# A hybrid decoder's state-space step rewritten: double-buffered scan rows, scans two quarters apart, weight remainders in halves

## The chip, the cores and the metric

The kernel runs on one core of a Trainium2 chip. The metric is device time in microseconds (us) of one execution, the median of a few runs. The engines are TensorE (PE in the profile, its weight loads PEld), VectorE (DVE), ScalarE (ACT), GpSimd (POOL) and SyncE (SP); each runs its own instructions in order and waits on counting semaphores.

## The reference, cut to what matters

One inference step of a hybrid decoder with 2 layers, model width 1024, over 512 prompt tokens and 8 x 4 sample tokens (544 columns in all), in float32. Each layer projects x, mixes a state-space branch with an attention branch, and adds an MLP. The change concerns the state-space branch (32 heads of 64, 8 groups, state 128, chunks of 128 tokens):

```python
xbc, conv_new = causal_depthwise_conv(xbc, conv_buf, conv_w, conv_b)   # width 4, then SiLU
dt = softplus(dt_raw + dt_bias); a = -exp(a_log)
acum = cumsum(dtc * a)                      # within a chunk
decay = exp(where(causal, acum_i - acum_j, -inf))
y_diag = einsum(cb * decay, x * dt)         # cb = C B^T in the chunk
states = einsum(B, x * dt * exp(acum_end - acum))
h <- h * exp(acum_end) + states             # chunk after chunk
y_off = einsum(C, h_prev) * exp(acum)
y = (y_diag + y_off + d_skip * x) * silu(z)
out = y * rsqrt(mean(y * y over a group) + eps) * norm_g
```

The sample tokens do the same from stored states (8 sequences, one chunk of 32 columns), which are updated and written out.

## The kernel before

Activations lie transposed, features on partitions and the 544 tokens on columns. A weight tile of 1024 x 128 is a **unit** (170 a layer), loaded by SyncE into a ring of four slots. For near-float32 products from fast passes ScalarE rounds it (`high`, L887, into `whi`), GpSimd takes the remainder (`low`, L1661, into `wlo`), and TensorE makes three products for each of eight slices and two column halves: high x high, high x low, low x high (L413, L414, L416). A unit is thus 48 matmuls of 272 columns, and each needs `low` of its unit (`w_split`) and, at the end, an eviction by ScalarE (`evac`, L894) that frees its accumulator.

Stages of a layer: the q, k, v projections, attention, **the state-space groups**, the merge of the branches with gates, the output projection, the MLP. In the groups' stage a step handles two groups at once: six units of group g are projected (B, C, two tiles of x, two of z) while the scan of group g - 1 runs in between. Step 0 has only the projection (the attention's sample tokens run in between), steps 1 to 7 have both, the last step has only the scan, with two units of the gates. `all_groups` calls `group(...)` once a step on every engine; steps 2 to 7 stand in a hardware loop of three rounds with two steps each.

TensorE's order is fixed: after every second slice of a unit (a **quarter**, 12 matmuls, 24 quarters a step) `between()` may insert a piece of the scan. `turn(c)` transposes chunk c's x and B into PSUM bank X[0] and makes C B^T there; `scan(c)` multiplies it out (L736, L739) and adds the chunk's state product (L748). Then come `turn_y`, `new_states` (L764), `rms` (L773) and `spread` (L780) at the quarters in the constants below.

VectorE's `chunk(k)` in order: C times decay (`cea`, L1434); from X[0] the rows x*dt (`xdt`, L1444), x*dt*decay (`xde`, L1445), B (`btok`, L1447) and the masked C B^T (`cbm`, L1451), which frees X[0]; the mask times the decays (`mdec`, L1455), which releases `scan(k)`; after that scan the state `hst` (L1465, four instructions). `conv(q)` is three taps (L1413) for each of four tiles, `silu(q)` L1420 and L1425; then `y_prompt` (L1477), `gate_z` (L1483), `y_sample`, `y_carried` (L1500), `gated_y` (L1505), `decay_states` (L1510) and `add_states` (L1516) for the samples, `norm_inverse` (L1520), `norm_scale` (L1525). ScalarE starts the convs (L1012), makes their tanh (L1018), the decays (`decay`, L1025 and L1029; `ea`, L1058), the squares (L1046) and the root (L1050). GpSimd, besides the remainders, pads each conv tile with its stored columns (`pad_of`, L1741 to L1744) and issues the loads and stores of states and tables.

The three orders that matter, as they stand:

```python
SCAN_AT = (3, 5, 8, 10, 12); Y_TURN_AT = 14; NEW_AT = 16; RMS_AT = 19; SPREAD_AT = 22
# TensorE: turn(0) of the next group waits for rs_ready, rms waits for sq_ready and ns_add
# VectorE: chunk(0) chunk(1) conv(0) chunk(2) chunk(3) y_prompt chunk(4) gate_z conv(1) silu(0)
#   y_sample y_carried gated_y silu(1) decay_states conv(2) add_states silu(2)
#   norm_inverse conv(3) silu(3) norm_scale
```

Of the kernel before, what the change touches and what calls it, by code (L numbers as in the profile page):

```python
# [30 lines left out]
P = 128  # L31
DEPTH, D = 2, 1024
SEQ, NB, NS = 512, 8, 4
TS = NB * NS
# [8 lines left out]
REG = 23840  # L43
# [33 lines left out]
SCAN_AT = (3, 5, 8, 10, 12)  # L77
Y_TURN_AT = 14
NEW_AT = 16
RMS_AT = 19  # L80
SPREAD_AT = 22
# [21 lines left out]
def build(nc, A):  # L103

    with ExitStack() as ctx:
# [55 lines left out]
        gconv = sb("gconv", [P, 20])  # L161
        gt = sb("gt", [P, NC + 1, 3, HG])
# [61 lines left out]
        xdt = reg.take(256)  # L224
# [5 lines left out]
        xde = reg.take(256)  # L230
        btok = reg.take(P)
# [15 lines left out]
        gates = reg.take(2, T)  # L247
        reg.restart(after_stores)
# [26 lines left out]
        def bc(ap, n):  # L275
# [30 lines left out]
        gp_ready, post_init, conv_done, th_ready, post_ready, spad_ready, thz_ready, zs_done = (  # L306
            sem(n) for n in ("gp_ready", "post_init", "conv_done", "th_ready", "post_ready", "spad_ready",
                             "thz_ready", "zs_done"))
        ea_ready, gt_ready, e_ready, t_done, x0_free, m_ready, y_done, h_ready = (
            sem(n) for n in ("ea_ready", "gt_ready", "e_ready", "t_done", "x0_free", "m_ready", "y_done", "h_ready"))  # L310
# [3 lines left out]
        ns_done, ns_add = (sem(n) for n in ("ns_done", "ns_add"))  # L314
# [68 lines left out]
        def _(pe):  # L383
# [138 lines left out]
            with pe.Fori(0, DEPTH) as L:  # L522
# [235 lines left out]
                def new_states(s):  # L758

                    pe.wait_ge(y_evac, 2 * s + 2)  # L760
                    for e in range(2):
                        for q in range(4):
                            rows = slice(32 * q, 32 * q + 32)
                            mm = nc.tensor.matmul(X[q][:, e * 256:(e + 1) * 256], bm[rows, e, :], xde[rows, :],  # L764
# [111 lines left out]
        def _(act):  # L876
# [67 lines left out]
            with act.Fori(0, DEPTH) as L:  # L944
# [59 lines left out]
                def group(g, s, unit0, rounds, late):  # L1004

                    c = None if g is None else L * GROUPS + g

# [960 lines left out]
```

## Time and profile before

| what | value |
|---|---|
| median of 3 runs | 3051.59 us (3051.0 to 3053.08) |
| the profiled execution | 3047.54 us |
| its span, first to last instruction | 3045.8 us |
| TensorE matmuls, weight loads busy | 2710.5, 2545.6 us (89%, 84%) |
| VectorE, ScalarE, GpSimd busy | 1296.3, 1087.7, 1052.0 us (43%, 36%, 35%) |
| mean granted TensorE clock | 0.944 |
| seven steps with scan and projection, a layer | 439.0 us |

The profiled execution is one run under the hardware profiler; the 1.7 us beside its span lie around the instructions. Busy shares are means over stages that differ. The granted clock is the share of full speed that the chip gave TensorE.

### The profile page before, as it was taken

The numbers are of one execution on the slowest core, as the hardware profiler recorded it, in microseconds if no ns is written. First come the engines' busy times: TensorE is split into PE (matmuls) and PEld (weight loads), VectorE is DVE, ScalarE is ACT, GpSimd is POOL, SyncE is SP. The second block draws the span as 40 slices with busy tenths as digits, with TensorE's granted clock in tenths as the row PEclk, the third lists the DMA queues.
The fourth block names the chain that finished last, engine by engine and source line by source line (L and its number), as shares of the span: only waits on it lengthen the run. The fifth ranks groups of instructions, "written<-read, shape, count | busy, mean of one in ns | idle before, by whom it ended". The sixth has DMA issues, their size and how long they took to land.

```text
span 3045.8 us, 53838 instructions
## 1 busy us (share of the span) xinstructions
PE 2710.5 (89%) x21264; PEld 2545.6 (84%) x21264; DVE 1296.3 (43%) x2064; ACT 1087.7 (36%) x1557; POOL 1052.0 (35%) x749
## 2 busy tenths in 40 slices
PE   5978888888889999999879798888887999999996
PEld 5966678788779989999879667778786999899996
DVE  4253367666641262011252524776676313520213
ACT  2232344455332243132232413445544322431323
POOL 3311233343233343434343012333332433433433
PEclk9989999999989999999989899999998999999998
DMA  3222322243222223222222232333333222223222
GB/s 118 83 101 95 108 94 96 94 137 107 89 72 83 88 70 90 84 89 90 70 74 81 86 118 92 97 101 123 108 96 102 74 88 81 75 84 90 86 88 78
DMA packets 66770, 280.47 MB, mean 92 GB/s; under 512 B 8384, under 2 KB 8832, under 8 KB 60064
## 3 DMA queue, kind: packets, MB, share of 16 engines
q1 hardware_dynamic: 51312, 184.51, 19.8%
q0 software_dynamic: 15280, 93.40, 8.5%
q8 instruction: 134, 2.20, 0.3%
q14 instruction: 44, 0.36, 0.0%
HBM read 248.81 MB, written 29.07 MB: 91 GB/s over the span
## 4 chain that ended last, share of the span: by engine, by line
PE 74%; DVE 15%; issue 3%; DVEq 3%; ACT 2%; ACTq 1%; DMA 1%; POOL 1%; POOLq 0%; SPq 0%
PE acc L413 19%; PE acc L414 19%; PE acc L416 19%; DVE region L1413 5%; PE px L736 1%; PE px L748 1%; PE acc L642 1%; PE px L677 1%; DVE region L1516 1%; PE px L597 1%; DVEq L1453 1%; PE acc L573 1%; DMA wring<-in_wst 1%; DVE region L1510 1%; PE acc L837 1%
## 5 line engine op out<-in xcount | busy, mean ns | idle before, releaser
L1661 POOL TENSOR_TENSOR wring_parts<-wring,whi 128x1024 fp32r<-128x1024 f32 x343 | 835.4, 2437 | 1063.3 <-ACT whi L887 1042.2
L413 PE MATMUL acc<-xhi,whi 128*128 128x272 f32 x3552 | 1008.6, 301 | 3.8 <-ACT big L948 2.7
L414 PE MATMUL acc<-xlo,whi 128*128 128x272 f32 x3552 | 974.9, 293 | 0.0
L416 PE MATMUL acc<-xhi,wring_parts 128*128 128x272 f32 x3552 | 746.6, 292 | 0.0
L413 PEld LDWEIGHTS acc<-xhi,whi 128*128 128x128 f32 x3552 | 686.3, 193 | 26.5 <-issue 19.6
L414 PEld LDWEIGHTS acc<-xlo,whi 128*128 128x128 f32 x3552 | 685.1, 193 | 3.5
L887 ACT ACTIVATE whi<-wring 128x1024 fp32r<-128x1024 f32 x343 | 362.0, 1056 | 888.1 <-DMA wring<-in_wst 797.3
L416 PEld LDWEIGHTS acc<-xhi,wring_parts 128*128 128x128 f32 x3552 | 566.9, 192 | 0.0
L413 PE MATMUL acc<-region_parts,whi 128*128 128x272 f32 x1792 | 487.3, 291 | 14.5 <-DVE big_parts L1585 14.5
L414 PE MATMUL acc<-big_parts,whi 128*128 128x272 f32 x1536 | 416.1, 289 | 0.0
L416 PE MATMUL acc<-region_parts,wring_parts 128*128 128x272 f32 x1792 | 372.2, 289 | 0.0
L413 PEld LDWEIGHTS acc<-region_parts,whi 128*128 128x128 f32 x1792 | 340.2, 190 | 16.0 <-issue 16.0
L414 PEld LDWEIGHTS acc<-big_parts,whi 128*128 128x128 f32 x1536 | 292.0, 190 | 0.0
L416 PEld LDWEIGHTS acc<-region_parts,wring_parts 128*128 128x128 f32 x1792 | 283.0, 190 | 0.0
L894 ACT ACTIVATE region<-acc 128x544 f32<-128x544 f32 x172 | 106.3, 618 | 395.4 <-PE acc L416 393.1
L1413 DVE SCALAR_TENSOR_TENSOR region<-region,gconv 128x600 f32<-128x600 f32 x192 | 205.3, 1069 | 19.7 <-ACT region L1012 6.2
L1625 DVE TENSOR_TENSOR region<-region 128x544 f32<-128x544 f32 x64 | 48.6, 760 | 269.9 <-ACT region_parts L1133 269.9
L1741 POOL COPY region<-region 128x32 f32<-128x32 f32 x64 | 29.2, 457 | 351.5 <-ACT region L894 347.4
L1018 ACT ACTIVATE region<-region 128x600 f32<-128x600 f32 x64 | 44.9, 702 | 183.1 <-DVEq L1415 183.1
L1025 ACT ACTIVATE region<-region,gt 128x128 f32<-128x128 f32 (+1 forms) x320 | 96.4, 373 | 15.2 <-DVE region L1455 11.0
L736 PE MATMUL px<-region 128*64 128x128 f32 (+1 forms) x640 | 63.2, 288 | 41.6 <-DVE region L1455 40.7
L1465 DVE SCALAR_TENSOR_TENSOR region<-region,px 128x64 f32<-128x64 f32 x192 | 41.1, 276 | 117.3 <-PE px L748 117.3
(233 smaller groups left out, 3104.5 us busy)
## 6 DMA issues: line engine op xcount, KB each, us to landing
wring<-in_wst SPq DMA_DIRECT2D x343, 512.0 KB, 3.6
region<-scratch_ac POOLq DMA_DIRECT2D x16, 1088.0 KB, 7.1
region<-in_st POOLq DMA_DIRECT2D x16, 1024.0 KB, 5.0
out_stout<-region POOLq DMA_DIRECT2D x16, 1024.0 KB, 9.0
big<-in_kc POOLq DMA_DIRECT2D x16, 768.0 KB, 5.6
big<-in_vc POOLq DMA_DIRECT2D x16, 768.0 KB, 5.7
out_kv<-region POOLq DMA_DIRECT2D x2, 3264.0 KB, 10.4
region<-in_x SPq DMA_DIRECT2D x1, 2176.0 KB, 8.4
```

The source lines that it names most:

```text
L413: nc.tensor.matmul(o, w_hi_, hi, start=first, stop=False)
L414: nc.tensor.matmul(o, w_hi_, lo, start=False, stop=False)
L416: mm = nc.tensor.matmul(out[:, 512 * h:512 * h + HT], w_lo_, parts(h)[0], start=False, stop=last)
L736: mm = nc.tensor.matmul(out, xdt[0:n, hcols], mdec[0:n, hh, 0:n], start=True, stop=c in (0, NC))
L887: nc.scalar.activation(whi[:, slot, :], whole[:, slot, :], ACT.Copy).then_inc(w_hi[slot], 1)
L894: nc.scalar.activation(halves(out), two(acc[b]), func, **kw).then_inc(acc_free[b], 1)
L1018: nc.scalar.activation(th[:, q % 2, 0:CONVW], pre[:, q % 2, 0:CONVW], ACT.Tanh).then_inc(th_ready, 1)
L1025: nc.scalar.activation(seg[0:n, k % 2, hh, 0:n], acb[0:n, hh, k * CHUNK:k * CHUNK + n], ACT.Relu, bias=gt[0:n, k, 1, hh:hh + 1], scale=-1.0)
L1413: nc.vector.scalar_tensor_tensor(v, raw[:, q, tap:tap + CONVW], gconv[:, 4 * q + tap:4 * q + tap + 1], v, ALU.mult, ALU.add)
L1465: ins = nc.vector.scalar_tensor_tensor(hst[:, hcols], hst[:, hcols], ea[:, hh, last:last + 1], X[3][:, hcols], ALU.mult, ALU.add)
L1625: nc.vector.tensor_tensor(v, v, v, ALU.mult)
L1661: pool.tensor_tensor(wlo[:, slot, :], whole[:, slot, :], whi[:, slot, :].bitcast(F32), ALU.subtract)\
```

## The change

Five things are done together. (1) The scan pieces stand at other quarters, `rms` and `spread` now ahead of `new_states`, and other waits go with them: `rms` no longer waits for `ns_add`, `turn(0)` of the next group does, `new_states` waits for `yssm_ready`. (2) `xdt`, `xde` and `btok` have two buffers each; a chunk is split into `rows_of` (what leaves X[0], and the decayed state `hdec`), `carry_state` of the chunk before, and `factors_of`. VectorE's and ScalarE's orders are rewritten; ScalarE makes the first two decays of the next scan at the end of a step. (3) The per-group copies `gt` and `gconv` are gone: the engines read `tokm` and `par` in place, `par` being halved once a layer. (4) The loop over steps is written out, so that slices are constants. (5) On GpSimd the remainders are made in halves of 512 columns (`low_half`), each behind a hold on an event of the scan, in a new order.

The constants and the loop over steps:

```diff
-SCAN_AT = (3, 5, 8, 10, 12)
-Y_TURN_AT = 14
-NEW_AT = 16
-RMS_AT = 19
-SPREAD_AT = 22
+SCAN_AT = (2, 4, 6, 8, 11)
+Y_TURN_AT = 13
+RMS_AT = 15
+SPREAD_AT = 18
+NEW_AT = 20
...
-            with eng.Fori(0, GROUPS // 2 - 1) as i:
-                group(2 * i + 2, first + 2 * i + 1, U_GRP + 12, 3 * i, True)
-                group(2 * i + 3, first + 2 * i + 2, U_GRP + 18, 3 * i, True)
+            for g in range(2, GROUPS):
+                group(g, first + g - 1, U_GRP + 6 * g, 0, True)
```

TensorE, in `turn`, `scan`, `new_states` and `rms`:

```diff
                         if late:
-                            pe.wait_ge(rs_ready, s)
+                            pe.wait_ge(ns_add, s)
...
+                    xdt, xde, btok = xdt2[c % 2], xde2[c % 2], btok2[c % 2]
                     pe.wait_ge(m_ready, 5 * s + c + 1)
-                    if c == 0 and late:
-                        pe.wait_ge(yssm_ready, 2 * s)
...
-                    pe.wait_ge(y_evac, 2 * s + 2)
+                    pe.wait_ge(yssm_ready, 2 * s + 2)
...
                     pe.wait_ge(sq_ready, s + 1)
-                    pe.wait_ge(ns_add, s + 1)
```

ScalarE; before, `decay(0)`, `ea` and `decay(1)` stood at a step's head. A step with scan and projection now runs: `zs`, decay(2), tile(0), decay(3), conv_init(0), decay(4), tile(1), conv_init(1), conv_act(0), copy_y, tile(2), conv_act(1), conv_init(2), square, root, tile(3), conv_act(2), conv_init(3), first_decay, conv_act(3), tile(4), rest_of_decay, tile(5).

```diff
+                    def first_decay():
+                        act.wait_ge(acb_ld, 16 * c + 16)
+                        if s is not None:
+                            act.wait_ge(m_ready, 5 * c)
+                        decay(0, g)
+
+                    def rest_of_decay():
+                        if s is not None:
+                            act.wait_ge(st_decayed, c)
+                        nc.scalar.activation(ea, acb, ACT.Exp).then_inc(ea_ready, 1)
+                        decay(1, g)
...
                 act.wait_ge(yssm_ready, 16 * L + 16)
+                act.wait_ge(ns_add, 8 * L + 8)
```

VectorE. A step now runs: chunks 0 to 3, conv(0), chunk(4), y_prompt, gate_z, conv(1), silu(0), y_sample, y_carried, gated_y, silu(1), conv(2), norm_inverse, silu(2), norm_scale, decay_states, conv(3), silu(3), add_states. `factors_of` holds what is left of the old chunk: `cea`, then `mdec`.

```diff
+                    def rows_of(k):
...
+                        dve.wait_ge(t_done, 5 * s + k + 1)
+                        xt = X[0][:, 0:256].rearrange("p (h d) -> p h d", h=HG)
+                        for out, j in ((xdt, 0), (xde, 2)):
+                            nc.vector.tensor_tensor(out.rearrange("p (h d) -> p h d", h=HG), xt,
+                                                    bc(tokm[:, k, j, gs * HG:(gs + 1) * HG], HD), ALU.mult)
...
+                        dve.drain().then_inc(x0_free, 1)
+                        if k > 1:
+                            last = k * CHUNK - 1
+                            nc.vector.tensor_tensor(hdec.rearrange("p (h d) -> p h d", h=HG),
+                                                    hst.rearrange("p (h d) -> p h d", h=HG),
+                                                    ea[:, :, last:last + 1].to_broadcast([P, HG, HD]), ALU.mult)
+                            dve.drain()
+
+                    def carry_state(k):
+
+                        dve.wait_ge(y_done, 5 * s + k + 1)
+                        if k > 0:
+                            nc.vector.tensor_tensor(hst, hdec, X[3][:, 0:256], ALU.add).then_inc(h_ready, 1)
+                        else:
+                            dve.wait_ge(h_free, s + 1)
+                            nc.vector.tensor_copy(hst, X[3][:, 0:256]).then_inc(h_ready, 1)
...
+                    def chunk(k):
+
+                        rows_of(k)
                         if k > 0:
+                            carry_state(k - 1)
+                        factors_of(k)
```

GpSimd. `last` is the unit that the third projection of the step uses; the units u to u + 4 plus AHEAD (3) are those after it. Behind the lines shown, the remainder of u + 1 + AHEAD waits for `m_ready` of chunk 4, the store of `hst` for `h_ready`, `load_decay` for `e_ready` (then pad 2, u + 2 + AHEAD, pad 3), u + 3 + AHEAD for `rs_spread`, u + 4 + AHEAD for the last `post_ready`, and the store of the sample states for `ns_add`.

```diff
+            def low_half(L, u, h):
+
+                slot, use = unit(L, u)
+                if h == 0:
+                    pool.wait_ge(w_hi[slot], use + 1)
+                cols = slice(h * KT * P // 2, (h + 1) * KT * P // 2)
+                ins = pool.tensor_tensor(wlo[:, slot, cols], whole[:, slot, cols], whi[:, slot, cols].bitcast(F32),
+                                         ALU.subtract)
+                if h == 1:
+                    ins.then_inc(w_split[slot], 1)
...
+                    if late:
+                        hold(pool, st_st, 16 * s)
+                        load_state(gs, s)
...
+                    last = U_GRP + 6 * gs + 5 + AHEAD
+                    for h in range(2):
+                        hold(pool, t_done, 5 * s + h + 1)
+                        low_half(L, last, h)
                     if projects:
                         pad_of(g, 0)
+                        for h in range(2):
+                            hold(pool, t_done, 5 * s + h + 3)
+                            low_half(L, u + AHEAD, h)
                         pad_of(g, 1)
...
```

## Rows read from the trace of the kernel before

**Rows 1.** The page: busy time; a group (busy, mean ns); a DMA issue.
```profile
PE 2710.5 (89%) x21264; PEld 2545.6 (84%) x21264; DVE 1296.3 (43%) x2064; ACT 1087.7 (36%) x1557; POOL 1052.0 (35%) x749
...
L1413 DVE SCALAR_TENSOR_TENSOR region<-region,gconv 128x600 f32<-128x600 f32 x192 | 205.3, 1069 | 19.7 <-ACT region L1012 6.2
...
out_stout<-region POOLq DMA_DIRECT2D x16, 1024.0 KB, 9.0
```

**Rows 2.** Windows: length, each engine's busy us (instructions), clock, DMA share, GB/s.
```profile
365.40:804.40 439.00, 378.82 (x3263) 352.40 (x3264) 302.64 (x553) 219.81 (x367) 158.25 (x161) 0.94 0.30 101
1873.70:2312.70 439.00, 379.77 (x3263) 353.62 (x3264) 303.37 (x553) 219.55 (x366) 157.91 (x161) 0.94 0.31 101
...
1123.00:1461.00 338.00, 337.46 (x2685) 337.20 (x2684) 61.82 (x81) 105.00 (x127) 139.36 (x61) 1.00 0.29 87
...
558.50:562.00 3.50, 3.50 (x17) 3.50 (x18) 1.84 (x5) 3.43 (x6) 0.56 (x1) 0.53 0.59 195
```

**Rows 3.** Waits of TensorE, 365.4 to 804.4: total us, times, longest.
```profile
PE px L773 <- DVE region L1516: 24.9, 7, 3.6
PE px L736 <- DVE region L1455: 17.1, 11, 2.3
...
PE px L711 <- DVEq L1453: 9.7, 7, 2.5
PE px L711 <- issue: 8.0, 2, 4.1
```

**Rows 4.** Timeline of VectorE, 505 to 575: start, us, instruction, [idle before].
```profile
509.04 2.85 DVE L1455 TENSOR_TENSOR region<-region 128x512 f32<-128x512 f32 x1
515.23 0.86 DVE L1465 SCALAR_TENSOR_TENSOR region<-region,px 128x64 f32<-128x64 f32 x4 [3.35 <-PE px L748]
...
517.87 0.69 DVE L1455 TENSOR_TENSOR region<-region 128x512 f32<-128x512 f32 x1
...
524.41 0.42 DVE L1444 TENSOR_TENSOR region<-px,gt 128x256 f32<-128x256 f32 x1
...
527.11 4.65 DVE L1413 SCALAR_TENSOR_TENSOR region<-region,gconv 128x600 f32<-128x600 f32 x3
...
533.95 1.29 DVE L1505 TENSOR_TENSOR region<-region 128x1088 f32<-128x1088 f32 x1
...
538.31 2.69 DVE L1413 SCALAR_TENSOR_TENSOR region<-region,gconv 128x600 f32<-128x600 f32 x3 [0.16 <-issue]
...
572.32 0.86 DVE L1465 SCALAR_TENSOR_TENSOR region<-region,px 128x64 f32<-128x64 f32 x4 [2.21 <-PE px L748]
```

**Rows 5.** Timeline of GpSimd, same stretch.
```profile
508.33 0.20 POOL L1742 COPY region<-cst 128x24 f32 x1
...
508.99 2.35 POOL L1661 TENSOR_TENSOR wring_parts<-wring,whi 128x1024 fp32r<-128x1024 f32 x1 [0.30 <-issue]
...
570.98 2.38 POOL L1661 TENSOR_TENSOR wring_parts<-wring,whi 128x1024 fp32r<-128x1024 f32 x1 [0.65 <-issue]
```

**Rows 6.** The chain that ended last, 440 to 505: start, us, what.
```profile
500.59 0.33 PE px L711 x3
...
502.21 0.64 PE px L748 x2
```

**Rows 7.** Timeline of ScalarE, 505 to 575.
```profile
535.27 1.11 ACT L1046 ACTIVATE region<-region 128x1088 f32<-128x1088 f32 x1 [1.61 <-DVE region L1505]
...
541.67 1.04 ACT L887 ACTIVATE whi<-wring 128x1024 fp32r<-128x1024 f32 x1
...
545.36 1.28 ACT L1050 ACT_TABLE_LOAD   x1
546.66 0.37 ACT L1050 ACTIVATE region<-px,eps 128x136 f32<-128x136 f32 x1
```

**Rows 8.** Timeline of ScalarE and GpSimd, 804 to 872.
```profile
850.61 8.86 ACT L1112 ACTIVATE region_parts<-big 128x544 fp32r<-128x544 f32 x16 [4.82 <-DVE big L1525]
...
849.65 0.54 POOL L1673 DMA_DIRECT2D wdt<-in_wdt  x1 [4.38 <-DMA out_stout<-region]
```

More of the change, by code:

```diff
@@ L42 @@
 CW = 4
-REG = 23840
+REG = 23880
 D_IN = HEADS * HD
@@ L223, in build @@
         cea = cea_flat.rearrange("p (h n) -> p h n", h=HG)
-        xdt = reg.take(256)
+        xdt2 = [reg.take(256) for _ in range(2)]
+        btok2 = [reg.take(P)]
         assert reg.at <= after_masks
@@ L247, in build @@
         gates = reg.take(2, T)
+        xde2.append(reg.take(256))
+        hdec = reg.take(256)
         reg.restart(after_stores)
@@ L1413, in conv @@
                             nc.vector.scalar_tensor_tensor(v, raw[:, q, tap:tap + CONVW],
-                                                           gconv[:, 4 * q + tap:4 * q + tap + 1], v, ALU.mult, ALU.add)
+                                                           par[:, g, 4 * q + tap:4 * q + tap + 1], v, ALU.mult, ALU.add)
                             dve.drain()
@@ L1543, in group @@
                     elif g is None:
-                        for k in range(NC):
+                        for k in range(NC + 1):
                             chunk(k)
                         y_prompt()
-                        chunk(NC)
                         gate_z()
@@ L1570, in group @@
                         silu(1)
+                        conv(2)
+                        norm_inverse()
+                        silu(2)
+                        norm_scale()
                         decay_states()
-                        conv(2)
-                        add_states()
-                        silu(2)
-                        norm_inverse()
                         conv(3)
                         silu(3)
-                        norm_scale()
+                        add_states()
                 all_groups(dve, L, group)
@@ L1750, in group @@
                     projects, scans = g is not None, s is not None
-                    if scans:
-                        if late:
-                            hold(pool, st_st, 16 * s)
-                            load_state(GROUPS - 1 if g is None else g - 1, s)
-                        if projects:
-                            hold(pool, cout_st, 16 * (L * GROUPS + g))
-                    if projects and not scans:
-                        pool.memset(raw[:, :, 0:PAD], 0.0)
+                    if not scans:
+                        pool.memset(raw[:, :, 0:PAD], 0.0)
+                        for q in range(4):
+                            pad_of(g, q)
+                        load_decay(g, L * GROUPS + g)
+                        load_state(g, L * GROUPS + g)
+                        low(L, u + 3 + AHEAD)
+                        low(L, u + 4 + AHEAD)
+                        return
@@ L1769, in group @@
+                        for h in range(2):
+                            low_half(L, u + 1 + AHEAD, h)
+                    hold(pool, h_ready, 4 * s + 4)
+                    pool.dma_start(row(A["hout"], s, "o p n -> (o p) n"), hst).then_inc(h_st, 16)
                     if projects:
+                        hold(pool, e_ready, 5 * s + 5)
+                        load_decay(g, L * GROUPS + g)
                         pad_of(g, 2)
-                        if scans:
-                            low(L, u + 2 + AHEAD, rounds)
+                        for h in range(2):
+                            low_half(L, u + 2 + AHEAD, h)
@@ L1789, in group @@
+                    hold(pool, ns_add, s + 1)
+                    pool.dma_start(row(A["stout"], s, "o p b n -> (o p) b n"), st).then_inc(st_st, 16)
+                    if not projects:
                         hold(pool, st_st, 16 * s + 16)
```

154 lines of the change are left out of this document (60 added, 94 removed).

## The prediction

> **What bounds the kernel now.** I read the page first: TensorE is busy 89% of the span [rows 1], so only stretches in which it is not can give time. The windows show which [rows 2]. In the feed-forward stretch it works without a gap at the full granted clock, 2685 matmuls in 338.0 us, 0.126 us each. The seven steps of the group loop that carry both a scan and a projection (groups 1 to 7, twice, once a layer) take 439.0 us a layer, 62.7 us each, at a mean granted clock of 0.94.
>
> How short could such a step be? It has 288 projection matmuls: 288 x 0.126 = 36.3 us. Between them stand the scan's own pieces. A step of turn and scan at full clock goes from 500.59 to 502.85, 2.26 us [rows 6]; there are three like it, and I put the other seven pieces, which carry fewer or shorter matmuls, at 1 us each (estimate from the same rows). Together 36.3 + 6.8 + 7.0 = 50.1 us. So 12.6 us per step are lost. The waits of TensorE say where [rows 3]: over seven steps 24.9 us at L773 (the squares' sum, which waits for the state update L1516), 17.1 at L736 and 9.7 at L711 (a scan and a turn, both for VectorE), 8.0 at the loop's back edge ("issue", 4.1 at the longest). That is 59.7 of the 88 us; the rest is the clock: after the wait at 558.5 the granted clock is 0.53, the lower of the two levels (1.2 and 2.4 GHz), for 3.5 us [rows 2].
>
> So TensorE waits for VectorE, although VectorE is busy only 302.64 / 439 = 69%, 43.2 us a step [rows 2]. Two things make it late. One is the order. The other is GpSimd: the multiply L1455 takes 0.69 us at 517.87 but 2.85 us at 509.04, where the remainder L1661 ran on GpSimd from 508.99 for 2.35 us; a conv triple takes 2.69 us at 538.31 and 4.65 us at 527.11 [rows 4, 5]. L1465, which reads PSUM, takes 0.86 us at 515.23 and the same at 572.32, amid a remainder that began at 570.98.
>
> **The change, part by part.** I set up one step with t = 0 at its first turn. A quarter is 12 matmuls, 1.51 us.
>
> *Scans two quarters apart.* Turn 3 starts after six quarters, turn 0 (0.55), turn 1 with scan 0 (2.26 less 0.5 for the state's matmuls) and turn 2 with scan 1 (2.26): 9.06 + 4.6 = 13.7, done at 14.2. Scan c needs, after scan c-1, one state add (0.4, the size of L1444), the C product and the mask multiply (0.7 each, one shape), 1.8 us of VectorE [rows 4], since the turned rows are now made beforehand in buffers of their own; TensorE spends 3.0 us on two quarters meanwhile. So I expect the waits at L711 and L736 to go, and cost the double buffers at nothing; their cover is 1.2 us, and a remainder half (below) can eat it. The four L1465 (0.86) become one product hdec and one add, about 0.8 with its drain.
>
> *VectorE from there to the gate.* Chunk 3 takes as long as now, 3.3 us from 515.23 to the end of 517.87's multiply. Then conv 0 (2.8), then chunk 4 up to the gated y: now 524.41 to 535.24 is 10.8 us; I take off the 1.96 that GpSimd added to the 4.65 conv, and add hdec with the carry (0.8) and y_prompt (1.4, now ahead of it): 11.1 [rows 4]. With 0.3 a time for a few handovers G, the end of the gate, is 14.3 + 3.3 + 2.8 + 11.1 + 0.8 = 32.3. TensorE reaches the squares' sum (quarter 15) at 22.6 + 11.1 (the pieces before it, by the same rows) = 33.8, and needs G plus the square (1.1 and a handover): even.
>
> *After the gate.* The new order releases the sum without the state update, so the wait at L773, 3.6 us a step, loses its reason. What is late next: silu 2 waits for its tanh, and ScalarE now has between them the square 1.1, a table load 1.28, the root 0.37, a weight copy 1.0, an eviction (0.6, put at that from its shape, half the square's), the load back 1.28 and the tanh (0.7, likewise): G + 6.4 with a handover [rows 7]. Then, by the rate of rows 4 (256 elements in 0.42, 1088 in 1.29: 0.15 us and 1.05 ns an element), silu 0.9, norm_scale 1.5, decay_states 2.3, conv 3 2.7, its tanh on ScalarE 0.8, silu 0.9, add_states 2.3: 11.4. I add 1.7 for a spread that comes late at the lower clock and a remainder half ahead of decay_states: 19.5. The next step's turn 0 waits for exactly that add (ns_add), and behind turn 0 stands the whole in-order projection. So a step is 32.3 + 19.5 = 51.8 us plus what GpSimd adds before G.
>
> The Trainium skill ("ScalarE: Activation LUTs", section "What ACT_TABLE_LOAD costs") puts a switch at 1283 ns of load and about 1380 ns of DRAIN. The trace agrees with the first figure alone: the load at 545.36 lasts 1.28 us and the root starts at 546.66. By the page's 2.66 us each step would be 2.8 us longer and the kernel 39 us; by the row it is not.
>
> *The remainders in halves.* The work is the same, 2.35 us a unit, and a second fixed cost: the smallest copies take 0.20 [rows 5], so a half is 1.2 to 1.3 us. Between t = 14 and G three units run, six halves, with two pads. Best case all fall on PSUM reads of VectorE: 0. Worst, each blocks a full 1.25: 7.5. Now the 12 conv taps of a step take 1.069 us on average [rows 1] against 0.90 (2.69 / 3), so GpSimd adds at least 2.0 a step. The holds on t_done do little for the first two units: GpSimd stands at the store of the sample states until it lands (9.0 us from issue [rows 1]), and by then those events are past. I take 2.7, near today's level. A step: 54.5 us.
>
> Against the change speaks that hdec reads two SBUF tiles where L1465 read PSUM: a new op that GpSimd can hold up, three times a step. The Trainium skill ("SBUF — State Buffer", section "SBUF: two separate sides") states it as a rule: the shared port pair goes to one of the two for the whole instruction when the VectorE op has two SBUF inputs. By it 3 x 1.25 = 3.8 us a step at worst, which is the third rival's price.
>
> *Queued behind the new waits.* On GpSimd, pad 0 and the remainders wait behind the stores' holds: unit 2's remainder is due at t = 21.5 and comes at about 13.5 (the store, the next load's issue, two halves), 8 us of cover. On ScalarE tile 4's eviction now stands behind conv 3's tanh, at t = 49, and is due at the next step's first projection, 2 us later; a longer VectorE chain moves both. In group 0, tile 4 waits for the first decay (five activations, the size of the root's 0.37 and one larger: 2 us [rows 7]), which delays the first projection of group 1: I take +2 us a layer.
>
> *Tables in place, loops written out.* gt and gconv, two VectorE ops of 60 and 20 columns, go; they lay in front of chunk 0, where TensorE did not wait for them. Two back edges a layer go, already counted in the 62.7. Halving par once costs one small VectorE op beside ScalarE's staging; without that cover 0.5 us.
>
> *Last step (no projection).* VectorE has no convs and the scans come sooner; adding the same lengths, ScalarE may start on the gated output about 39 us after the first turn, against 46.2 now (850.61 - 804.4) [rows 8]. GpSimd's next remainders still wait for the store of the states (landed at 849.65 now), so I take 6 of the 7: -12 us for both layers.
>
> **Sum.** 14 steps x (62.7 - 54.5) = 115; + 12 - 4 = 123 us. The profiled execution took 3047.5 us: 2924.5. The median of the runs is 4 us above it: **2928 us**.
>
> **Rivals.** (1) TensorE bound: GpSimd falls into PSUM reads and waits, c near 0, a step of 51: 14 x 11.7 + 8 = 172, 2880 us. For it: VectorE's 43 us fit; against: no slack is left anywhere. (2) Contention as priced by the worst half of the range, or hdec held up each time: a step of 58, 14 x 4.7 + 8 = 74, 2978 us. For it: the 2.85 and 4.65 us rows. (3) The waits only move, from L773 to the same sum waiting for the gate and to turn 0: a step of 60, 46 us, 3006 us. (4) Slower: turn 0 on ns_add closes a ring through VectorE's whole work; if the 22.6 us of GpSimd (158.25 / 7) nearly all stand in its way, 43.2 + 20 = 63 to 64 us a step, 3062 us; it decides from 11 us of contention a step, four times what I take.
>
> **Numbers.** Chances: my forecast 0.45, (1) 0.22, (2) 0.20, (3) 0.07, (4) 0.06. The range takes in the steps from 50 to 59 us, all but (3) and (4): 2866 to 2990. 0.2%, 6 us, is about what a measurement can tell from no change. Faster 0.94, same 0.01, slower 0.05.
>
> **What would show it.** Right: no wait at the back edges; no or short waits at scans and turns 1 to 4; the sum's wait under 3.5 us and released by ScalarE's square; turn 0 of each step released by the state add; a mean granted clock above 0.94 in the steps; steps of 53 to 56 us. Wrong: turn 0 waiting for nothing (then rival 1); conv taps above 1.07 us on average (rival 2); a projection waiting for its remainder or for an eviction, which would break the cover I gave to GpSimd's and ScalarE's queues.

## The result, and the profile after

The changed kernel took 2938.44 us (median of 4 runs, 2934.34 to 2943.11); the kernel before took 3051.3 us beside it (4 runs, 3037.03 to 3053.08). The ratio is 0.964, with a 95% interval of 0.9608 to 0.9673: faster, and 10 us above the 2928 that was forecast, inside the range. The profiled execution took 2938.64 us, with a span of 2937.1.

The windows of the seven steps of each layer, to be held against the first two of [rows 2]:

```profile
364.20:753.90 389.70, 365.38 (x3263) 340.95 (x3264) 297.45 (x497) 222.27 (x369) 172.47 (x202) 0.97 0.32 113
1818.20:2207.70 389.50, 365.21 (x3263) 340.75 (x3263) 296.79 (x497) 222.30 (x370) 172.67 (x202) 0.97 0.32 113
```

The step went from 62.7 to 55.7 us (779.2 / 14), at a mean granted clock of 0.97 in place of 0.94, with the same 3263 matmuls. The two stretches give 98.8 us. The waits of TensorE over the whole execution show what is left (columns as in [rows 3]; over the whole execution of before, L773 had 57.7 us in 16 waits, L736 40.7 in 23, the two waits at L711 20.2 and 16.2):

```profile
PE px L771 <- ACT region L1046: 36.9, 16, 3.5
...
PE px L711 <- DVE region L1544: 13.7, 14, 1.0
...
PE acc L413 <- POOL wring_parts L1678: 6.7, 2, 3.4
...
PE px L735 <- DVE region L1490: 4.6, 5, 1.1
PE acc L413 <- ACT region L892: 3.6, 4, 1.2
```

The wait for the state update at the squares' sum has gone; the sum (now L771) waits for ScalarE's square L1046 instead, up to 3.5 us. Scans (now L735) wait 4.6 us in all. The back edges are no longer in the list. Each step's turn 0 (L711) waits for the state add L1544, 0.97 us as a rule. The page's lines for VectorE's conv, GpSimd's halves and ScalarE's conv_init:

```profile
L1687 POOL TENSOR_TENSOR wring_parts<-wring,whi 128x512 fp32r<-128x512 f32 x172 | 272.8, 1603 | 217.0 <-issue 74.4
...
L1426 DVE SCALAR_TENSOR_TENSOR region<-region,par 128x600 f32<-128x600 f32 x192 | 206.6, 1076 | 36.8 <-ACT region L1011 23.2
...
L1011 ACT ACTIVATE region<-region,par 128x600 f32<-128x600 f32 x64 | 56.5, 882 | 88.4 <-POOLq L1773 88.4
```

The conv taps are as slow as before (1076 ns against 1069 in [rows 1]): there, contention with GpSimd has not gone down. And a line that was not foreseen: L1011 waits 88.4 us for L1773, the drain behind GpSimd's pad copies. The chain that ended last shows what that does. One step's second half (start, us, what):

```profile
729.04 3.75 POOLq L1773
...
732.82 0.89 ACT region L1011
733.70 1.01 ACT region L1046
...
734.76 0.96 PE px L771 x16
...
736.24 0.23 PE acc L414
...
741.66 0.94 PE px L778 x8
...
744.10 2.20 DVE region L1538
...
746.49 1.59 DVE region L1426
...
748.16 0.84 DVE region L1426
...
749.99 0.71 ACT region L1017
...
750.73 0.69 DVE region L1433
...
751.52 2.21 DVE region L1544
...
753.87 0.30 PE px L711
```

Read it from the top. GpSimd's queue is at the drain for 3.75 us; then ScalarE can do conv_init, and only behind it, in order, the square; then the sum. The matmuls after the sum, behind TensorE's wait, take 0.23 us each until 738.65, where the full granted clock has 0.126 [rows 2]. The windows before and after that moment have the granted clock (third figure from the end): 0.53, the lower level, and 1.00:

```profile
735.70:738.60 2.90, 2.90 (x15) 2.90 (x14) 2.71 (x3) 1.62 (x3) 0.26 (x1) 0.53 0.00 0
738.70:741.60 2.90, 2.90 (x25) 2.90 (x24) 0.24 (x1) 2.87 (x4) 1.08 (x4) 1.00 0.57 178
```

So the spread at L778 is late twice over: by the sum's delay, and by the matmuls at the lower clock. From there it is VectorE's series to the state add and turn 0, as forecast, with conv taps of 1.59 among those of 0.84.

Why is the drain so long? GpSimd and ScalarE in the step from 644.09 to 698.57:

```profile
668.55 3.59 POOL L1687 TENSOR_TENSOR wring_parts<-wring,whi 128x512 fp32r<-128x512 f32 x2 [2.80 <-DVE region L1490]
...
672.64 0.54 POOL L1758 DMA_DIRECT2D region<-scratch_ac  x1
...
675.59 0.21 POOL L1772 COPY region<-region 128x35 f32<-128x35 f32 x1
679.11 3.05 POOL L1687 TENSOR_TENSOR wring_parts<-wring,whi 128x512 fp32r<-128x512 f32 x2 [3.31 <-issue]
```
```profile
679.01 0.89 ACT L1011 ACTIVATE region<-region,par 128x600 f32<-128x600 f32 x1 [3.57 <-POOLq L1773]
679.81 1.09 ACT L1046 ACTIVATE region<-region 128x1088 f32<-128x1088 f32 x1
680.92 1.28 ACT L1050 ACT_TABLE_LOAD   x1
682.21 0.37 ACT L1050 ACTIVATE region<-px,eps 128x136 f32<-128x136 f32 x1
```

The pad's last copy ends at 675.80, yet ScalarE is released at 679.01. What stands ahead in GpSimd's queue is the load of the decay table, issued at 672.64. The view of that one load (L1758, 672 to 674) has its landing:

```profile
DMA to landing us min/median/max: 6.2/6.2/6.2
```

That is at 678.85, and the drain ends at 678.98. It is so in every step. The traces of the changed kernel, of its second run and of e2 to e10 have 213 pads at whose last copy a load issued by GpSimd was still under way: each drain ended 0.13 to 0.21 us after that load had landed, and the landings came from 5.0 to 8.3 us after the issue. So the drain goes by the landing, not by a time of its own. The load in its turn stands behind a pair of halves that took 3.59 us.

The last step of a layer, where ScalarE starts on the gated output (before: 46.2 us after the first turn, [rows 8]):

```profile
793.94 8.88 ACT L1123 ACTIVATE region_parts<-big 128x544 fp32r<-128x544 f32 x16 [4.69 <-DVE region L1544]
```

That is 40.1 us after its first turn at 753.87, 6.2 us sooner than before (6.17 from unrounded times), twice. With the 98.8 from the steps that makes 111.1; the profiled executions differ by 3047.5 - 2938.64 = 108.9, so some 2.2 us were lost elsewhere: from that start to the next layer's first turn 0, and to the end, the changed kernel is 1.2 and 2.4 us longer, and ahead of the first turn 0 it is 1.2 us shorter. The wait for a remainder in the list above (L413 for L1678, 3.4 us a layer, in the merge) is new, but no loss: with the 8.0 us for VectorE there it makes 14.7, and before TensorE waited 14.5 there for VectorE alone.

### The profile page after: what moved, and what is told of

The parts are those of the page before. It is cut to its first block, busy times and chain, and to the rows that moved or that the text cites. A ratio compares the mean times of both kernels' runs of the same rounds, so it can differ in the third digit from the quotient of the medians.

```text
span 2937.1 us, 53722 instructions
## 1 busy us (share of the span) xinstructions
PE 2681.7 (91%) x21264; PEld 2521.7 (86%) x21264; DVE 1275.6 (43%) x1938; ACT 1070.1 (36%) x1545; POOL 1080.1 (37%) x835
## 4 chain that ended last, share of the span: by engine, by line
PE 77%; DVE 11%; ACT 3%; issue 2%; POOLq 2%; POOL 1%; ACTq 1%; DMA 1%; DVEq 1%; SPq 0%
PE acc L413 20%; PE acc L414 20%; PE acc L416 19%; DVE region L1426 2%; POOLq L1773 2%; PE px L677 1%; PE acc L642 1%; PE px L735 1%; PE px L747 1%; DVE region L1544 1%; PE px L597 1%; PE acc L573 1%; DVE region L1538 1%; PE acc L458 1%; PE acc L835 1%
## 5 line engine op out<-in xcount | busy, mean ns | idle before, releaser
L413 PE MATMUL acc<-xhi,whi 128*128 128x272 f32 x3552 | 999.6, 299 | 6.9 <-ACT region L892 3.6
L1678 POOL TENSOR_TENSOR wring_parts<-wring,whi 128x1024 fp32r<-128x1024 f32 x257 | 625.2, 2435 | 978.2 <-ACT whi L885 973.3
L413 PEld LDWEIGHTS acc<-xhi,whi 128*128 128x128 f32 x3552 | 677.6, 191 | 29.7 <-issue 22.5
L413 PE MATMUL acc<-region_parts,whi 128*128 128x272 f32 x1792 | 488.7, 291 | 14.8 <-DVE big_parts L1602 8.0
L413 PEld LDWEIGHTS acc<-region_parts,whi 128*128 128x128 f32 x1792 | 341.2, 190 | 17.5 <-issue 10.3
L1687 POOL TENSOR_TENSOR wring_parts<-wring,whi 128x512 fp32r<-128x512 f32 x172 | 272.8, 1603 | 217.0 <-issue 74.4
L1426 DVE SCALAR_TENSOR_TENSOR region<-region,par 128x600 f32<-128x600 f32 x192 | 206.6, 1076 | 36.8 <-ACT region L1011 23.2
L1025 ACT ACTIVATE region<-region,tokm 128x128 f32<-128x128 f32 (+1 forms) x320 | 96.2, 372 | 19.6 <-DVE region L1490 19.6
L1448 DVE TENSOR_TENSOR region<-px,tokm 128x256 f32<-128x256 f32 x160 | 60.6, 420 | 98.3 <-PE px L717 94.5
L1011 ACT ACTIVATE region<-region,par 128x600 f32<-128x600 f32 x64 | 56.5, 882 | 88.4 <-POOLq L1773 88.4
L1651 DVE SCALAR_TENSOR_TENSOR region<-region,acc 128x544 f32 x16 | 11.5, 721 | 175.8 <-PE acc L416 175.8
```

Source lines behind the costliest of these rows:

```text
L413: nc.tensor.matmul(o, w_hi_, hi, start=first, stop=False)
L1011: nc.scalar.activation(pre[:, q % 2, 0:CONVW], raw[:, q, PAD:RAWW], ACT.Identity, bias=par[:, g, 16 + q:17 + q], scale=par[:, g, 4 * q + 3 ...
L1025: nc.scalar.activation(seg[0:n, k % 2, hh, 0:n], acb[0:n, hh, k * CHUNK:k * CHUNK + n], ACT.Relu, bias=tokm[0:n, k, 1, head:head + 1], sca ...
L1426: nc.vector.scalar_tensor_tensor(v, raw[:, q, tap:tap + CONVW], par[:, g, 4 * q + tap:4 * q + tap + 1], v, ALU.mult, ALU.add)
L1448: nc.vector.tensor_tensor(out.rearrange("p (h d) -> p h d", h=HG), xt, bc(tokm[:, k, j, gs * HG:(gs + 1) * HG], HD), ALU.mult)
L1678: pool.tensor_tensor(wlo[:, slot, :], whole[:, slot, :], whi[:, slot, :].bitcast(F32), ALU.subtract)\
```

## The experiments

All times are ratios to the kernel before, run on the same chip. "Step" is the mean over the 14 steps that scan and project. Kernels e2 to e10 are edits of the changed kernel, e1 of the kernel before.

**The loop alone (e1).** Before, with the groups' loop written out:

```diff
-            with eng.Fori(0, GROUPS // 2 - 1) as i:
-                group(2 * i + 2, first + 2 * i + 1, U_GRP + 12, 3 * i, True)
-                group(2 * i + 3, first + 2 * i + 2, U_GRP + 18, 3 * i, True)
+            for g in range(2, GROUPS):
+                group(g, first + g - 1, U_GRP + 6 * g, 0, True)
```

> The kernel before with one part of the change alone: the loop over steps 2 to 7 written out. My theory: the four back edges (two a layer) cost 4.1 us of idle TensorE each and some 1.7 us more at the lower clock after it, so this alone is 23 us faster than before, ratio 0.992, with no wait on 'issue' left at L711. Rival: written-out code has to be fetched just the same, the wait turns up elsewhere: ratio 1.000.

Measured: 0.9925 (0.9901 to 0.9949). No back edge is left among the waits, and the sum's wait is what it was (57.8 us in 16). The loop is worth 0.75% by itself.

**Whole remainders (e2), halves without their holds (e3), no remainder at all (e4).** In e2 each pair of halves is one whole remainder; where each half had its own hold, it stands behind both. e3 keeps the halves and drops the five waits that release them. e4 fills the halves with zeros: TensorE's work stays, the group products lack this part, and GpSimd reads nothing.

```diff
 e2 (at four places so; at the first two the holds of both halves stay ahead of it)
-                        for h in range(2):
-                            low_half(L, u + 1 + AHEAD, h)
+                        low(L, u + 1 + AHEAD)
 e3
-                        hold(pool, t_done, 5 * s + h + 1)
-                            hold(pool, t_done, 5 * s + h + 3)
-                        hold(pool, m_ready, 5 * s + 5)
-                        hold(pool, rs_spread, s + 1)
-                        hold(pool, post_ready, 4 * (L * GROUPS + g) + 4)
 e4
-                    pool.wait_ge(w_hi[slot], use + 1)
+                    hold(pool, w_hi[slot], use + 1)
...
-                ins = pool.tensor_tensor(wlo[:, slot, cols], whole[:, slot, cols], whi[:, slot, cols].bitcast(F32),
-                                         ALU.subtract)
+                ins = pool.memset(wlo[:, slot, cols].bitcast(F32), 0.0)
```

> The changed kernel with whole remainders (1024 columns) at the same releases, halves undone. My theory: a remainder in VectorE's way now blocks up to 2.4 us where a half blocks 1.25, about 1 us more a step in the ring from turn 3 to the state add: 14 us slower than the changed kernel, ratio to before 0.969. Rival 1: the lock's total is the same, nothing changes: 0.964. Rival 2: the halves are what made the ring short, 4 us a step: 56 us slower, 0.982.

> The changed kernel with the halves not held back by scan events (the holds on t_done, m_ready, rs_spread and post_ready ahead of the remainders are gone). My theory: the t_done holds are past when GpSimd comes to them and the others move a half by little: within 10 us of the changed kernel, ratio to before 0.961 to 0.967. Rival: the holds keep GpSimd out of VectorE's two-input work; without them 3 us a step, 42 us slower, 0.978.

> The changed kernel with the halves of the remainder replaced by a fill with zeros, which reads no SBUF (the remainders of the weights used in the groups' stage are left out of the products). My theory: GpSimd costs the ring 2.7 us a step; with that gone the conv triples fall to 2.7 us each, a step to 52.5 to 53 us, the kernel by 38 to 45 us, ratio to before 0.950. Rival: the ring is set by ScalarE's chain and handovers, VectorE has the room to take GpSimd's blocks: 10 us at most, 0.961.

Measured: e2 0.9648 (0.9616 to 0.9681), e3 0.9619 (0.9588 to 0.9651), e4 0.9492 (0.9462 to 0.9523). Neither halving nor the releases gave anything beyond the uncertainty of the comparison; my 14 us for halving fell. e4 came out as expected, with a step of 52.2 (51.4 to 51.5 for most). What is left at turn 0 and at the sum is 0.2 us each time and 13.8 us in 16, half of that in the two last steps:

```profile
PE px L771 <- ACT region L1046: 13.8, 16, 3.4
...
PE px L711 <- DVE region L1544: 3.2, 14, 0.2
```

So the remainders cost 3.4 us a step. (A fill takes GpSimd 0.53 us and a half 1.29, medians, so e4 takes away GpSimd's time as well as the contention.) To see where, take mean ns of one instruction from VectorE's groups, for the operations that read SBUF alone (of `mdec` the four prompt chunks); the column before the last is their busy time beyond e4's, over the execution:

| kernel | conv L1426 | silu L1433 | hdec L1460 | cea L1481 | mdec L1490 | gate_z L1511 | gated L1533 | decay L1538 | beyond e4, us | step, us |
|---|---|---|---|---|---|---|---|---|---|---|
| e4 | 867 | 692 | 427 | 684 | 737 | 1285 | 1293 | 2285 | 0 | 52.2 |
| after | 1076 | 691 | 460 | 764 | 887 | 1285 | 1292 | 2284 | 55 | 55.7 |
| e2 | 880 | 861 | 755 | 716 | 943 | 2227 | 1292 | 3243 | 74 | 55.4 |
| e3 | 867 | 1447 | 654 | 1110 | 994 | 1284 | 1323 | 2285 | 96 | 54.7 |
| e6 | 995 | 690 | 510 | 709 | 841 | 1284 | 3440 | 2285 | 71 | 56.1 |
| e8 | 867 | 1356 | 663 | 1233 | 770 | 1285 | 3316 | 2284 | 115 | 58.5 |
| e9 | 871 | 692 | 466 | 684 | 737 | 1284 | 1296 | 2446 | 5 | 52.3 |

e3 has 41 us more contention than the changed kernel and is no slower. What an instruction is held up by counts only where the step has no slack. Ahead of the gate VectorE's wait for the turned y makes up for it: 0.37 us of that wait are left in the changed kernel, 1.4 in e4 (medians), and the gated y starts 32.1 us after turn 0 in both; in e3 part of the delay gets through, and it starts at 32.9. Between gate and state add nothing makes up for it.

**The quarters (e5).** The changed kernel with the old places of turns and scans:

```diff
-SCAN_AT = (2, 4, 6, 8, 11)
-Y_TURN_AT = 13
-RMS_AT = 15
-SPREAD_AT = 18
-NEW_AT = 20
+SCAN_AT = (3, 5, 8, 10, 12)
+Y_TURN_AT = 14
+RMS_AT = 16
+SPREAD_AT = 19
+NEW_AT = 21
```

> The changed kernel with the scan pieces back at the old distances (3, 5, 8, 10, 12; then 14, 16, 19, 21), all engines' orders as changed. My theory: VectorE's serial stretch starts at turn 3, which moves from quarter 6 to quarter 8, 3.0 us later, and the ring to the state add is full, so a step grows by 2 to 3 us: 28 to 42 us slower than the changed kernel, ratio to before 0.974 to 0.978. Rival: the order on VectorE is the whole gain, TensorE's quarters have room: 0.964.

Measured: 0.9845 (0.9811 to 0.988), a step of 59.6: right in sign, and about twice the size expected. The rows of turn 3 start 18.5 us after turn 0 instead of 14.4 (medians of L1448), and the step is 3.9 us longer, so all four microseconds arrive at the end. VectorE does not use the time: it waits for each turn, and the new waits are at the end of the ring:

```profile
PE px L771 <- ACT region L1046: 54.8, 16, 5.3
PE px L711 <- DVE region L1544: 34.8, 14, 2.5
```

**The load of the decay table behind pad 2 (e6), the state add ahead of silu 3 (e7).**

```diff
 e6
+                        pad_of(g, 2)
                         hold(pool, e_ready, 5 * s + 5)
                         load_decay(g, L * GROUPS + g)
-                        pad_of(g, 2)
 e7
                         conv(3)
+                        add_states()
                         silu(3)
-                        add_states()
```

> The changed kernel with one move on GpSimd: the load of the next decays is issued after pad 2 instead of ahead of it. In the changed kernel's trace the drain behind pad 2 takes 3 us longer than behind pad 1, with that load issued 2.4 us before it, and ScalarE's conv start 2 and then the square wait for it (the square starts at 679.8 where its input was there at 678.3). My theory: the drain waits for the load's descriptors; without it the square starts some 1.2 us earlier and a step is 0.9 to 1.2 us shorter: 13 to 17 us faster than the changed kernel, ratio to before 0.959. Rival: the drain is late because VectorE holds the port during conv 1; the move does nothing: 0.964.

> The changed kernel with VectorE's state add ahead of silu 3, so that it runs while ScalarE makes the tanh that silu 3 waits for (0.8 us). My theory: the ring from the gate to the next turn 0 is full (each turn 0 waits 0.97 us for the state add), so the step shrinks by what is hidden, 0.8 us: 11 us faster than the changed kernel, ratio to before 0.9605. Rival: the wait at turn 0 only takes over what the squares' sum lost, and nothing is gained: 0.964.

Measured: e6 0.9718 (0.9686 to 0.9751), e7 0.9654 (0.9619 to 0.9689). In e6 the drain is short, as the theory of the queue said: the copies end at 678.37, ScalarE is released at 678.54. But now the two halves start at the moment of the gate:

```profile
678.16 0.21 POOL L1772 COPY region<-region 128x35 f32<-128x35 f32 x1
679.15 0.54 POOL L1758 DMA_DIRECT2D region<-scratch_ac  x1 [0.78 <-issue]
679.71 2.53 POOL L1687 TENSOR_TENSOR wring_parts<-wring,whi 128x512 fp32r<-128x512 f32 x2
...
691.18 4.60 POOL L1687 TENSOR_TENSOR wring_parts<-wring,whi 128x512 fp32r<-128x512 f32 x2 [1.42 <-PE px L778]
```
```profile
679.62 3.77 DVE L1533 TENSOR_TENSOR region<-region 128x1088 f32<-128x1088 f32 x1
...
690.96 1.47 DVE L1553 SCALAR_TENSOR_TENSOR big<-region,par,px 128x544 f32<-128x544 f32 x2 [0.43 <-PE px L778]
692.35 2.29 DVE L1538 TENSOR_TENSOR region<-region 128x2048 f32<-128x2048 f32 x1
```

The gated y takes 3.77 us instead of 1.29 (3.7 to 3.9 in all 14 steps); the 2.48 beyond are the two halves (2.53), all of them, though by the rows it begins 0.09 us ahead of them. The square is as late as before, for another reason. (The execution in the trace, 2944.4 us, is the fastest of e6's four; their median is 2953.6, so the rows need not show the whole loss.) Mechanism right, but for what the drain waits for (the load's landing and not its descriptors), and gain false: the long drain had kept GpSimd out of the way of the gate. Further down the same rows show the other side of it: decay_states, at 692.35, takes its 2.29, and it is the pair of halves begun at 691.18 that takes 4.60. norm_scale at 690.96, which reads PSUM, takes its 1.47 beside them.

The Trainium skill ("SBUF — State Buffer", section "SBUF: two separate sides") says that the port pair shared by VectorE and GpSimd is an exclusive lock held for a whole instruction, not a split of bandwidth, and that a VectorE operation with two SBUF inputs needs it against a GpSimd operation that reads SBUF. The rows above agree (2.48 beside 2.53). e4 agrees with the last condition: its fills read nothing, and a gated y takes 1.29 us though two of them run beside it:

```profile
504.03 0.99 POOL L1687 MEMSET wring_parts<- 128x512 f32 x2 [1.47 <-issue]
```
```profile
503.88 1.29 DVE L1533 TENSOR_TENSOR region<-region 128x1088 f32<-128x1088 f32 x1
```

In e7 the wait of turn 0 for the state add is gone, and the sum waits 44.1 us (5.7 at the longest) instead of 36.9: the rival was right, the ring closes elsewhere.

**All of it at once (e8).** e3, e6 and e7 together, with group 0's first decay behind tile 4's eviction and the merge's first remainders ahead of the hold on the store of the states:

```diff
+                        tile(4)
                         first_decay()
-                        tile(4)
 ...
+                        low(L, U_MRG + AHEAD)
+                        low(L, U_MRG + 1 + AHEAD)
```

> Both moves of the two kernels before this one, the remainders' holds gone, group 0's first decay behind its tile 4, and the merge's first two remainders ahead of the wait for the last state store. My theory: a step comes down by 1.2 and 0.8 us to 52.5, near TensorE's own 51.4 that the run without remainders showed; 2 us less in groups 0 to 1 and 6 us less at the merge (the 3.4 us wait for a remainder, once a layer): 50 us faster than the changed kernel, ratio to before 0.947. Rival: GpSimd's blocks grow elsewhere, as the steps of the unheld run (54.2) are bound by the turns: 15 us, 0.959.

Measured: 0.9789 (0.9758 to 0.9821): slower than the changed kernel. Without holds the halves run as soon as they can, and with the load moved that is the gate, a scan's factors, and silu 2 (see the table; one silu took 3.13). At the merge the wait for the remainder became one for VectorE, longer than both had been (changed kernel: 8.0 and 6.7 us):

```profile
PE acc L413 <- DVE big_parts L1602: 18.0, 2, 9.0
```
```profile
690.79 3.59 DVE L1533 TENSOR_TENSOR region<-region 128x1088 f32<-128x1088 f32 x1
...
700.73 3.13 DVE L1433 SCALAR_TENSOR_TENSOR region<-region 128x512 f32<-128x512 f32 x1 [1.92 <-ACT region L1017]
```

So taking the causes away one at a time fails as long as the halves have to fall somewhere. That left one theory: there is enough VectorE time that is PSUM reading or waiting to hold all twelve halves.

**The changed kernel again, and halves placed in VectorE's windows (e9, e10).** e9 releases each half by an event behind which VectorE reads PSUM or waits (the five turns, the last mask, silu 0, the root, the reciprocal, the spread, silu 3), two in a row only where VectorE's add from PSUM is long enough, puts the load behind pad 2, and waits for the store of the states after two halves. All products are kept. e10 also moves group 0's first decay behind tile 4.

```diff
-                    if late:
-                        hold(pool, st_st, 16 * s)
-                        load_state(gs, s)
...
+                        hold(pool, t_done, 5 * s + 3)
+                        low_half(L, u + AHEAD, 0)
...
+                        hold(pool, t_done, 5 * s + 4)
+                        low_half(L, u + AHEAD, 1)
+                        hold(pool, t_done, 5 * s + 5)
+                        low_half(L, u + 1 + AHEAD, 0)
...
+                        low_half(L, u + 1 + AHEAD, 1)
+                        hold(pool, post_ready, 4 * c + 1)
+                        low_half(L, u + 2 + AHEAD, 0)
+                        pad_of(g, 2)
...
+                        hold(pool, rs_ready, s + 1)
+                        low_half(L, u + 2 + AHEAD, 1)
+                        hold(pool, rs_inv, s + 1)
+                        low_half(L, u + 3 + AHEAD, 0)
```

> The changed kernel once more, beside the next two on one chip: ratio to before 0.964 (0.961 to 0.967), steps of 55 to 56 us.

> The changed kernel with each of the twelve halves of a step released by an event after which VectorE reads PSUM or waits: the five turns (rows_of), m_ready of chunk 4 (y_prompt), silu 0 (y_sample, y_carried), the root (reciprocal), the reciprocal (wait for the tanh), the spread (norm_scale), silu 3 (the state add, two halves); the states' store is awaited after two of them and not ahead of all, and the load of the decays is issued behind pad 2. All products are kept. My theory: GpSimd's blocks after the gate, 3.9 us a step between the changed kernel and the run without remainders, fall below 1 us; a step of 51.5 to 52.5 us, conv triples of 2.7 us, ratio to before 0.949 to 0.953. Rival: events come late or the pads and the stores' issue push the halves out of their windows, as in the two kernels with the load moved; 0.960 to 0.970.

> The kernel before this one, and in group 0 the first decay behind tile 4 and not ahead of it. My theory: the first projection of group 1 no longer waits 1.24 us for the eviction of tile 4, once a layer: 2.5 us faster than the kernel before this one, below what the times can tell; the wait of L413 for L892 is gone from the trace. Rival: the first chunk's mask then waits for the decay, and the 2.5 us come back at scan 0.

Measured, on one chip: the changed kernel 0.966 (0.964 to 0.9679), e9 0.9507 (0.9488 to 0.9526; 2891.3 us), e10 0.9514 (0.949 to 0.9537). The first two came out as expected. e9 beats both kernels, by 1.6% the changed one (0.9507 / 0.966), and does all the work as fast as e4 leaves it out. Its waits, its conv taps, a stretch of six steps, and two of its halves beside what VectorE did:

```profile
PE px L771 <- ACT region L1046: 14.4, 16, 3.5
...
PE px L711 <- DVE region L1544: 5.8, 14, 0.6
```
```profile
L1426 DVE SCALAR_TENSOR_TENSOR region<-region,par 128x600 f32<-128x600 f32 x192 | 167.3, 871 | 20.6 <-ACT region L1011 7.1
```
```profile
417.70:727.20 309.50, 304.94 (x2796) 284.87 (x2797) 230.83 (x426) 187.74 (x313) 122.91 (x175) 1.00 0.37 129
```
```profile
653.76 1.29 POOL L1687 TENSOR_TENSOR wring_parts<-wring,whi 128x512 fp32r<-128x512 f32 x1 [4.92 <-DVE region L1438]
...
660.41 1.44 POOL L1687 TENSOR_TENSOR wring_parts<-wring,whi 128x512 fp32r<-128x512 f32 x1 [2.94 <-ACT region L1050]
```
```profile
653.50 0.40 DVE L1517 SCALAR_TENSOR_TENSOR region<-region,par,px 128x32 f32<-128x32 f32 x2
655.23 0.78 DVE L1528 TENSOR_TENSOR region<-region,px 64x32 f32<-64x32 f32 x4 [1.33 <-PE px L754]
...
660.82 1.00 DVE L1548 RECIPROCAL region<-region 128x136 f32<-128x136 f32 x1
```

The half at 653.76 fills the time in which VectorE has a PSUM read and then waits 1.33 us for the turned y; that at 660.41 runs beside the reciprocal of one input and the wait behind it. Step: 51.6 us (309.5 / 6), clock 1.00.

In e10 the waits of 1.24 us for tile 4's eviction are gone, as expected, and the first step of a layer is 1.1 and 0.9 us shorter (54.0 against 55.1 in the first); but two of its later steps took 56.6 and 55.0 us, and its total is no better. No run tried why, but the traces point to it, and to where e9's windows end. The load of the sample states waits for their store; behind the load stand pad 0, whose drain goes by the load's landing, and the next halves. Counted from turn 0, the load lands at 15.2 and 14.7 us in these two steps and at 14.95 in the one long step of e9 (53.9); in the 21 other steps with such a load, all 51.6, it lands between 11.7 and 14.65.

## Why the prediction was right, and where it was off

- *TensorE waited for VectorE's order.* Right. The waits at the scans went (17.1 us over seven steps to 4.6 over both layers), and turn 3's rows start at 14.4 us, where the working had the turn done at 14.2. By e5 the places of the scan's pieces, given the rest of the change, are worth 0.9845 - 0.966 = 2% of the kernel, the largest part, and they set when the gate comes, microsecond for microsecond. Double buffers, orders and tables in place were not taken back one by one: with the old places they and the loop together make 1.55%, of which the loop alone makes 0.75.
- *The uncontended step, 51.8 us.* Right in size: 52.2 in e4, 52.3 in e9. That it is so close is partly luck, since its parts erred in opposite senses: the gate's end came 33.4 us after turn 0 and not 32.3, and what follows took some 18 in e4's steps of 51.4, not 19.5.
- *2.7 us of contention ahead of the gate.* This is the step that failed. The gated y starts 32.1 us after turn 0 with remainders and without (medians in the changed kernel and e4): contention there costs nothing, the wait for the turned y takes it up. The cost is 3.4 us (55.66 - 52.24; 3.8 between the medians), and it lies after the gate, where I had put 1.7 for a late spread and one half together. That 2.7 and 3.4 are near each other is luck. Most of it is not the port but GpSimd's time: the halves delay the load (issued 27.7 us after turn 0, 25.1 in e4), the drain ends only when the load has landed, ScalarE's conv_init waits for the drain, and the square stands behind that. The sum starts at 36.6 instead of 34.6; at the lower clock the spread falls back a further 1.0; conv 3 adds 0.75 by contention. That I named ScalarE's queue and GpSimd's queue as the covers to watch was right; the drain was not in my list.
- *L773 loses its reason, near even.* The releaser changed as forecast; it was even only in e4 and e9 (about 0.5 us a step: 14.4 less two of 3.5 in the last steps, over 14), not in the changed kernel.
- *Turn 0 released by the state add; back edges; table load of 1.28.* Right, each: 0.97 us at L711 as a rule, 0.75% by e1, and the root 0.01 us behind the load's end (680.92 + 1.28, 682.21).
- *The holds do little; hdec may be held up three times a step.* e3 bears out the first for all five. hdec took 460 ns against 427 in e4; held by whole remainders (e2) 755, still without effect on the time. The working calls that price the third rival's; it stands in the second.
- *Group 1's first projection, 2 us a layer.* The wait is 1.24, for tile 4's eviction. The whole first step of a layer is 3.5 us longer than the others (55.1 against 51.6 in e9); the rest stands behind an 11.6 us wait at turn 0, with a mean granted clock of 0.95 against 1.00.
- *The last step, 6 us.* 6.2.
- *Sum.* Forecast: 115 + 12 - 4 = 123; measured: 98.8, which holds group 1's wait, + 12.3 - 2.2 = 108.9. The steps are short of the 115 by 16: in each of the 14, contention and GpSimd's time took 3.4 instead of 2.7, and the uncontended step 0.4 more than forecast.
- *The sign I had set for rival 2*, conv taps above 1.07 us on average, does not tell the cases apart: the changed kernel has 1.076, e2 0.880 and the same time. Rival 1's step of 51 could nearly be had (51.6 for most), by e9, not by this change. A third sign showed too: a projection waiting for its remainder, 3.4 us a layer in the merge, behind a remainder that took 5.76 us at 801.3 where others take 2.4; it did not make the merge's waits longer.

Open: what the double buffers, the orders and the tables in place are worth one by one; why the store of the sample states lands late in some steps; what the 2.2 us lost outside the steps were spent on.

## What to carry to other kernels

GpSimd's work beside VectorE has no price per microsecond: the same remainders cost 0, 3.4 or 6.3 us a step (e9, the changed kernel, e8), by whether they, or what queued behind them, fell on a stretch with slack. Find the series that has none (here gate to state add), list the PSUM reads and waits of VectorE inside it, and release one short piece of GpSimd work into each; splitting the work without choosing the events gave nothing here. A drain that another engine waits for belongs ahead of GpSimd's own loads, but only with the next pieces placed as well (e6 lost by the move alone, e9 has both). And when a wait is removed, look at what it had been keeping apart.

## What the runs showed of the hardware

- A drain on GpSimd ended only when a load that GpSimd itself had issued before it had landed: 0.13 to 0.21 us after the landing in all 213 cases, with landings 5.0 to 8.3 us after the issue. A semaphore that such a drain raises is late by as much. With the load behind the drain the release came 0.17 us after the last copy (e6).
- A VectorE operation with two SBUF inputs that meets two GpSimd halves can be held for both of them, 3.77 us in place of 1.29 (e6); a GpSimd fill held up nothing (1.29 in e4). Operations that read PSUM kept their time beside halves: `norm_scale` 1.47 us for two, the state add 2.28 in the changed kernel's 14 steps.
- The lock goes either way: beside decay_states it was GpSimd that waited (4.60 us for two halves, 2.53 elsewhere).
